# A ring of eight weight slots and rounds of eight experts in a hybrid decoder step

## The reference, cut to what matters

```
g_idx  = argmax(xf @ w_group + b_group)              # one of 4 groups
top 2 of the 8 experts of that group, by xf @ w_router + b_router
def expert_block(a):                                  # for each of the 32 experts
    gate, up = split(xb @ w_gate_up[e], 2)            # 1024 x 1024
    return (silu(gate) * up) @ w_down[e]              # 512 x 1024
y = sum over a token's two experts of weight * row
```

## Time and profile before

| what | value |
|---|---|
| median of 3 runs | 2447.42 us |
| the profiled execution's own time | 2444.9 us |
| its span | 2443.2 us |
| PE busy | 1804.6 us, 74% |
| DMA | 604.27 MB, mean 247 GB/s |
| experts of layer 0, on PE | 861.5 to 1420.2 us |
| experts of layer 1, on PE | 1868.4 to 2402.2 us |

### The profile page before, as it was taken

The page is one execution under the profiler, slowest core; times in us unless marked ns, Lnnn a source line. Parts: engine busy times, 40 slices in busy tenths (PEclk is TensorE's granted clock), DMA queues, the critical chain, the costliest instruction groups (busy, mean ns, idle before and its releaser), DMA issues. The chain is left out here.

```text
span 2443.2 us, 26085 instructions
## 1 busy us (share of the span) xinstructions
PE 1804.6 (74%) x8637; PEld 846.2 (35%) x8638; DVE 487.0 (20%) x989; ACT 300.4 (12%) x563; POOL 179.7 (7%) x167
## 2 busy tenths in 40 slices
PE   3779877368867478888888718999944788787682
PEld 1335333134433333333333204555442333332231
DVE  0010695332132201100000031121131010000003
ACT  1130111322101010010101012000020101010001
POOL 0000111001102200000000030000121000000004
PEclk8769989568688589999999968999967999899896
DMA  7992203907701277799999990010045999999994
GB/s 252 387 383 72 69 18 104 351 30 238 285 22 69 91 301 272 297 407 410 408 411 411 410 342 2 1 69 2 35 172 215 354 366 411 409 411 411 411 410 174
DMA packets 194115, 604.27 MB, mean 247 GB/s; under 512 B 15951, under 2 KB 18288, under 8 KB 193897
## 3 DMA queue, kind: packets, MB, share of 16 engines
q1 hardware_dynamic: 158064, 522.21, 55.1%
q10 hardware_dynamic: 25761, 46.50, 5.2%
q0 software_dynamic: 10208, 34.48, 4.0%
HBM read 551.57 MB, written 52.01 MB: 247 GB/s over the span
## 5 line engine op out<-in xcount | busy, mean ns | idle before, releaser
L780 PE MATMUL ps<-ring,W 128*64 128x512 f32 x2048 | 465.4, 605 | 55.5 <-issue 32.7
L793 PE MATMUL ps<-ring,W 128*64 128x512 f32 x1024 | 272.8, 680 | 52.0 <-DVE W L1591 47.2
L780 PEld LDWEIGHTS ps<-ring,W 128*64 128x64 f32 x2048 | 173.2, 139 | 335.7 <-issue 334.9
L909 ACT ACTIVATE W<-ps 128x512 f32<-128x512 f32 (+4 forms) x243 | 134.5, 568 | 973.5 <-PE ps L793 364.3
L1585 DVE TENSOR_TENSOR W<-W,ps 128x256 f32<-128x256 f32 x64 | 26.9, 421 | 796.4 <-ACT W L1175 796.4
L886 PE MATMUL ps<-hT,ring 128*128 128x512 f32 x384 | 170.7, 597 | 0.5 <-DVE W L1609 0.5
L793 PEld LDWEIGHTS ps<-ring,W 128*64 128x64 f32 x1024 | 91.0, 155 | 193.3 <-issue 193.3
L545 PE MATMUL ps<-ring,hT 128*128 128x512 f32 (+1 forms) x240 | 116.9, 646 | 1.9 <-DVE W L1292 1.9
L467 PE MATMUL ps<-ring,cT 128*32 128x512 f32 x384 | 75.8, 931 | 31.9 <-DMA ring<-in_w_ada_dram 31.7
L886 PEld LDWEIGHTS ps<-hT,ring 128*128 128x128 f32 x384 | 71.1, 190 | 80.9 <-issue 80.4
L1304 DVE SCALAR_TENSOR_TENSOR W<-W,prm 128x512 f32<-128x512 f32 x120 | 89.5, 817 | 0.0
(11 more groups left out here) (280 smaller groups left out, 1553.4 us busy)
## 6 DMA issues: line engine op xcount, KB each, us to landing
ring<-in_w_gate_up_dram SPq DMA_DIRECT2D x128, 2048.0 KB, 16.8
ring<-in_w_down_dram SPq DMA_DIRECT2D x64, 2048.0 KB, 17.0
ring<-in_w_ada_dram SPq DMA_DIRECT2D x24, 2048.0 KB, 19.7
x_rows<-X ACTq DMA_DIRECT2D x1, 18944.0 KB, 53.0
ring<-in_cache_k_dram SPq DMA_DIRECT2D x64, 256.0 KB, 3.0
W<-x_rows SPq DMA_DIRECT2D x32, 512.0 KB, 17.8
x_rows<-W ACTq DMA_DIRECT2D x128, 128.0 KB, 5.9
ring<-in_cache_v_dram POOLq DMA_DIRECT2D x48, 256.0 KB, 4.6
```

Source lines behind the costliest of these rows:

```text
L780: x = mm(ps[CAP * z:CAP * z + CAP, 2 + j, :], xt[:, k, :], at[:, :, 256 * z:256 * z + 256], start=(k == 0), stop=(k == KD - 1))
L793: x = mm(ps[CAP * z:CAP * z + CAP, 5 + j, :], ht[:, k % 2, CAP * (k // 2):CAP * (k // 2) + CAP], ring[:, 3 * j + 2, at:at + 512], start=(k ...
L909: return fn(out, src, ACT.Copy, **k)
```

## The change

The ring gets two more slots, `slots[6]` and `slots[7]`, of the same size, laid over the first 4096 columns of `Hb` and of `hT`. Parts go round the eight slots: part k of expert i of a round lies in slot (3 i + k) mod 8, which closes after 8 experts. So the loop of each engine becomes 4 rounds of 8 steps, without a written-out last round, and SP loads a part when the part eight places before it has been used. The two new slots get their first parts (expert number 2 of the order, its two gate/up halves) once the scatter has landed and the logits are made. To have no special last step, there is a 17th pair of rows in `x_rows`, which is fetched and turned and not used (PAIRS 17, and the region behind the experts starts P rows later, XB). The gate of the sample rows moves to `g2s`, in columns 4096 to 5119 of `Hb`. The six loads of w_in_c wait for the last users of slots 0 to 5 in the new order.

```diff
-PAIRS = E // 2
+PAIRS = E // 2 + 1
+XB = E * CAP + P
-XR = -(-(E * CAP + (XTRA + NB - 1) * XC) // P) * P
+XR = -(-(XB + (XTRA + NB - 1) * XC) // P) * P
+NRING = 8
+LOADS = 3 * E // NRING
+        slots = [ring[:, s, :] for s in range(NSLOT)] + [hflat[:, 0:SLOT], tflat[:, 0:SLOT]]
+        g2s = hflat[0:NS, SLOT:SLOT + D]
...
-            with eng.Fori(0, E // 4 - 1) as q:
-                quad(q)
-            quad(E // 4 - 1, last=True)
+            with eng.Fori(0, E // 8) as r:
+                for i in range(8):
+                    p, q = 4 * r + i // 2, i // 2 + 1
+                    step(8 * r + i, i, r, p, i // 2 % 2, (q % 2, 2 * r + q // 2, 4 * r + q) if i % 2 else None)
+
+        def place(i, k):
+            return divmod(3 * i + k, NRING)
...
+                def fetch(r, i, parts=(0, 1, 2)):
+                    for k in parts:
+                        before, part_before = divmod(3 * i + k - NRING, 3)
+                        sp.wait_ge(M[("g0_mm", "gu_mm", "down_mm")[part_before]], done(l, 8 * r + before))
+                        part(EG * (i % 4) + 2 * r + i // 4, k, place(i, k)[1])
+                        if k == 1 and i % 2 == 0:
+                            rows_in(4 * r + (i // 2 + 1), (i // 2 + 1) % 2)
...
                 layer_wait(sp, l, "disp", 32 * NT)
                 rows_in(0, 0)
                 rows_in(1, 1)
-                step(0, 0, 2 * EG, pair=(2, 0))
...
-                with sp.Fori(0, 6) as q:
-                    quad(q)
-                quad(6, last=True)
-                step(E - 3, 1, E - 1)
+                layer_wait(sp, l, "lg_mm", 1)
+                part(2 * EG, 0, 6)
+                part(2 * EG, 1, 7)
+                rows_in(2, 0)
+                fetch(0, 2, (2,))
+                for i in range(3, 8):
+                    fetch(0, i)
+                with sp.Fori(1, E // 8) as r:
+                    for i in range(8):
+                        fetch(r, i)
...
-                def landed(j, k, p):
-                    pe.wait_ge(slot_in[3 * j + k], p * 16 + (base_in[l][3 * j + k] + 16))
+                def landed(r, i, k):
+                    turn, s = place(i, k)
+                    pe.wait_ge(slot_in[s], r * 48 + (base_in[l][s] + 16 * turn + 16))
```

More of the change, by code:

```diff
@@ L213, in mod @@
             return modT[:, MODS * KD * l + KD * m:MODS * KD * l + KD * m + KD, :]
-        slot_in = [sem(f"slot_in{s}") for s in range(NSLOT)]
+        slot_in = [sem(f"slot_in{s}") for s in range(NRING)]
         v_in = [sem(f"v_in{j}") for j in range(2)]
@@ L250, in hybrid_step @@
         seq = 16 * NPG
-        in0 = [80 + 5 * seq] * 2 + [80, 80, 96, 80]
-        in1 = [in0[s] + 16 * PAIRS + (32 if s < 2 else 16) for s in range(NSLOT)]
+        in0 = [80 + 5 * seq] * 2 + [80, 80, 96, 80] + [0, 0]
+        in1 = [in0[s] + 16 * LOADS + (32, 32, 16, 16, 16, 16, 0, 0)[s] for s in range(NRING)]
         base_in = [in0, in1]
@@ L373, in experts @@
                         sp.wait_ge(S["bch_mm"], 4 * (s // 3 + 1))
-                    part(EG * (s // 3), s // 3, s % 3)
+                    part(EG * (s // 3), s % 3, s)
                 def rows_in(p, j):
@@ L392, in experts @@
                 rows_in(1, 1)
-                step(0, 0, 2 * EG, pair=(2, 0))
[L395 to L399, removed]
-                with sp.Fori(0, 6) as q:
-                    quad(q)
-                quad(6, last=True)
-                step(E - 3, 1, E - 1)
[L406 to L409, removed]
+                layer_wait(sp, l, "lg_mm", 1)
[8 more added lines that the diff above has]
+                        fetch(r, i)
             experts(0)
             winc = a["w_in_c"][0].rearrange("(k p) n -> p k n", p=P)
[L413 to L416, removed]
+            for s in range(NSLOT):
+                last, part_last = divmod(3 * E - NRING + s, 3)
+                sp.wait_ge(M[("g0_mm", "gu_mm", "down_mm")[part_last]], done(0, last))
+                col = D * (s % 3) + 512 * (s // 3)
+                load(s, winc[:, :, col:col + 512])
             woutc = a["w_out_c"][0].rearrange("(k p) n -> p k n", p=P)
@@ L774, in ffn, with gate_up @@
                 layer_wait(pe, l, "gate2_ev", 4)
-                def gate_up(xt, j, half, signal):
+                def gate_up(xt, i, half, signal):
+                    j, slot = i % 2, slots[place(i, half)[1]]
                     for k in range(4 * half, 4 * half + 4):
-                        at = ring[:, 3 * j + half, D * (k % 4):D * (k % 4) + D].rearrange("p (g f) -> p g f", g=2)
+                        at = slot[:, D * (k % 4):D * (k % 4) + D].rearrange("p (g f) -> p g f", g=2)
                         for z in range(2):
@@ L787, in h_turns, with down @@
                     x.then_inc(signal, 1)
-                def down(ht, j, signal):
+                def down(ht, i, signal):
+                    j, slot = i % 2, slots[place(i, 2)[1]]
                     for k in range(FE // P):
@@ L793, in down @@
                             x = mm(ps[CAP * z:CAP * z + CAP, 5 + j, :], ht[:, k % 2, CAP * (k // 2):CAP * (k // 2) + CAP],
-                                   ring[:, 3 * j + 2, at:at + 512], start=(k == 0), stop=(k == FE // P - 1))
+                                   slot[:, at:at + 512], start=(k == 0), stop=(k == FE // P - 1))
                     x.then_inc(signal, 1)
                 def pair_turns(lane, count, p):
-                    pe.wait_ge(x_in[lane], count * 16 + (16 * (PAIRS // 2) * l + 16))
+                    pe.wait_ge(x_in[lane], count * 16 + (16 * ((PAIRS + 1 - lane) // 2) * l + 16))
                     pe.wait_ge(M["xa_ok"], pdone(l, p - 1))
@@ L819, in one_pass @@
                         for half in range(2):
-                            landed(j, half, p)
+                            landed(r, i, half)
                             carry(pe)
                             for k in range(4 * half, 4 * half + 4):
-                                at = ring[:, 3 * j + half, D * (k % 4):D * (k % 4) + D].rearrange("p (g f) -> p g f", g=2)
+                                at = slots[place(i, half)[1]][:, D * (k % 4):D * (k % 4) + D].rearrange(
+                                    "p (g f) -> p g f", g=2)
                                 for z in range(4):
@@ L837, in one_pass @@
                                 x = mm(ps[XC * z:XC * z + XC, 5 + j, 0:256], hhT2[:, k, :],
-                                       ring[:, 3 * j + 2, at:at + 256], start=(k == 0), stop=(k == 3))
+                                       slots[place(i, 2)[1]][:, at:at + 256], start=(k == 0), stop=(k == 3))
                         x.then_inc(F["products"], 1)
@@ L1707, in ffn, with step @@
                 meet(pool, k0)
-                def step(n, j, p, lane, nxt=None):
+                def step(n, i, r, p, lane, nxt=None):
+                    j = i % 2
                     def one_pass(c):
```

58 lines of the change are left out of this document (23 added, 35 removed).

## The result

The changed kernel takes 2541.3 us (median, 2528.8 to 2546.0) against 2446.6 us (2438.1 to 2448.9) of the kernel before on the same chip: ratio 1.0386, interval 1.0337 to 1.0434. It is 95 us slower; 50 were forecast. The profiled execution spans 2544.2 us against 2443.2.

A forecast was written before the change was run, and what follows sets the result against it. It took DMA as setting the loops' pace (16.7 us an expert where it is the limit), PE close behind. Code stalls of 83.8 less 33.9 us of weight waits gave +50 on the profiled 2444.9, so 2497 us predicted, range 2420 to 2545.

The forecast's parts named there:

- The place of the decision: PE's code in the expert loops: a round of eight, 11 packets, is not kept and every round fetches it again.
- rival B: Much slower by code alignment: four stalls in a round instead of two, 66 us more, 2563 us; chance 0.10.
- the forecast's own case: Rounds of eight fetched again each time: 2497 us, from 2447 to 2535; chance 0.62.
- idle at issue, apart from jumps back: PE's code-fetch stalls within rounds of both loops: 12 more at 2.85 us, +34.2 us.
- six jumps back: PE's returns to the loop head, three a layer: 5.7 us each, 17.1 us a layer.
- longer products: PE's slow product behind each added stall: 1.28 us on the mean, none counted for jumps back.
- waits for weights: PE's waits for late weights in both loops go nearly whole: 8 + 25.9 = 33.9 us saved.
- two such stalls: In each round of eight on PE, one stall per half: 8 a layer against 2 before.
- the price of one: Each stall on PE in fresh code: 2.85 us idle plus 1.28 us of slower product, 4.1 us.
- What the ring is worth: Two more weight slots put DMA 10.2 us further ahead; alone worth 8 + 16.5 = 24.5 us.
- The small parts: 17th pair, x_rows fill, SP's new order and gate's new place: 0.1 us a layer for transposes, otherwise 0.
- ACT's, DVE's and POOL's longer rounds: Their code fetches on queue 14: unpriced, from 0 to one 2.85 us stall per jump back, taken as 0.

The follow-up runs named there:

- e1: Changed kernel with the ring put back to six slots, rounds of eight kept: 2533.7 us.
- e2: Changed kernel with further-pass code left out on the engines at steps where this input needs none, valid for this input only: 2397.4 us.
- e4: Kernel before with 56 never-executed products added to each step on PE, a round then 9.3 packets: 2770.2 us.
- e5: e2 with a ring of six slots instead of eight: 2435.5 us.
- e12: e6 with no instruction changed, TensorE's two loops moved to begin at the start of a packet: 2428.5 us.
- e9: Changed kernel with hint_back_edge=True on TensorE's loop, one instruction more at each round's head: 2511.1 us.
- e6: e2 with further-pass code at four steps of the round instead of two, the added ones never entered: 2468.1 us.
- e8: Kernel before with a one-column Silu on ACT ahead of the products' wait at each round's first step: 2439.1 us.
- e3: Kernel before with further-pass code kept at only one step of four in each layer: 2435.5 us.
- e11: Kernel before with the last four experts as an eighth round, an unused 17th pair, and e8's early Silu: 2425.6 us.
- e10: Changed kernel with further-pass code moved behind the round and reached by branches, valid for any routing: 2505.2 us.

## Why the prediction was right, and half as large as the effect

**The place of the decision was right.** The forecast stood on one step: a round of eight is about 11 packets, TensorE doesn't keep it, and each round fetches it again. It named 11 to 12 packets a round and some 130 in all; 13 (11 and 12 in the first rounds) and 127 came. e1, e2 and e4 show the cause: without the far slots nothing changes, without the unused code 144 us go, and with unused code added to TensorE alone the kernel before loses 326 us. That 11 packets are too many, and that they go out in the order in which they came in, was my assumption; no row of before shows either. The runs put the step between 5.8 and 7.6 packets. The kernel before, e5 and e2 jump back over 5.8, 5.7 and 5.7 packets without a fetch: none in 945 to 1350 us, in 1020 to 1391 us of e5, in 1006 to 1391 us of e2. A round that touches seven stays (e2, 37 packets), one that touches eight does not (e12, 96 packets).

**The number is half luck.** 2541.3 lies in the range, whose end of 2545 was drawn for rival B's sake; it lies above 2535, the high end of the forecast's own case, and the measured loss is almost twice the forecast's. The errors of the terms below mostly point the same way.

**The terms.** Over both loops, forecast and measured by the profiled executions:

| term | forecast | measured |
|---|---|---|
| idle at issue, apart from jumps back | +34.2 (12 more at 2.85) | +56.1 (32.7 to 88.8, 19 more) |
| six jumps back | +34.2 (5.7 each) | +55.4 (9.2 each) |
| longer products | +15.4 | +29.2 |
| waits for weights | -33.9 | -37.6 |
| waits for DVE before the second turn | 0 | -11.2 |
| the rest of the loops | 0 | +4.0 |
| sum | +50 | +95.9 |

**The number of stalls failed first.** "A round of eight has two such stalls": the price of one held, the number did not. The list of waits had 13 idle times at issue in the two loops before. Nine of them stand directly behind a further pass, one behind each of the nine experts that take one, as ahead of the product at 1225.52 in the earlier trace rows:
```profile
1220.82 1.94 PE L837 MATMUL ps<-ring,W 128*32 128x256 f32 x32 [0.38 <-DVE W L1577]
```
Seven of these nine fall in rounds whose code was all there, so they are no fetches, and the same nine are all that e2 has. The other four, 2.85 us each, are the four passages through fresh code of the earlier trace rows. In the changed kernel the nine are there again (24.0 us against 21.3), and apart from them and the jumps back there are 23 of 2.8 us. The forecast had two a round, 16; there were 2.9 a round. Rival B, with 2563 closer to the time than the forecast, had four a round, 32 in all; 23 is nearer to 16. Why it is about three was not tested.

**The jump back was mis-sized.** "I take the nearest rows, two idle times of 2.85": it is 9.2 us, above both the 5.7 taken and the 8.3 that I had as the upper end. e9 bears out that it is the fetch of the head: in four of six, where one packet was left in the idle time instead of two, 3.2 to 3.8 us were left.

**The longer products are the third.** PE's busy time rose by 29.2 us, of which the unused pair's turns are 2.2 (two times eight in 1.09 us). The rest, 27.0 us over 19 more stalls and six jumps back, is 1.1 us for each; the forecast took 1.28 for 12 stalls and nothing for the jumps, behind which all six products are slow. e6 and e12 show that this term isn't fixed by the number of packets, since it moved by 20 us in one loop with the fetches unchanged.

**What the ring is worth** where the code stays came out higher, 32 to 38 us instead of 24.5 (e5 against e2). The changed kernel has nothing of it: with PE so slow, six slots are enough (with six, e1, it takes 2534 us; with eight 2541). The waits for weights that the forecast took off go with either ring.

**The table loads were missed.** The forecast did not see that ACT loads its table once a round. The waits before the second turn fell by 11.2 us, 8.0 of it by six loads fewer (2.47 against 1.14). In the changed kernel, where PE sets the pace, this counts in full; in the kernels with short code it doesn't: moving all 14 loads is worth 5 to 9 us (e8), and e5 with six loads fewer is level with e3.

**The small parts held.** The first refill went out at 854 us, right behind the row fetches, and nothing of the SP's new order is seen in PE's waits. ACT's, DVE's and POOL's longer rounds, which I left unpriced, cost little: queue 14 has 64 packets instead of 33, and PE's waits for DVE before `down` (L790, L793 before) are 49.7 us instead of 47.2. The first product of layer 1 had an idle time of 5.87 at issue, counted above with the stalls.

## What to carry to other kernels

Count the packets that a loop's instructions touch, with code that is jumped over, before unrolling it further. On TensorE, in these runs, a round that touched seven (5.8 packets long) was free from the second time on, one that touched eight (7.6 long) was fetched whole in every round; nothing between was run. The step was worth 31 to 71 us by where the code lay (e12, e6), as much as or more than the 32 to 38 that two more slots of weights brought. Code written out once behind a loop is fetched too, five packets in layer 0; with a dummy turn in its place and the early table load, the kernel was 25 us faster than before (e11).

## What the runs showed of the hardware that was not expected

- A round that is too long by a packet or two is not one fetch dearer: all of it is fetched, 9 packets for a round of 7.6 (e6, e12).
- A jump back to a head that is gone costs 8.4 to 9.6 us of idle time (the changed kernel, e6's and e12's layer 1), an entry to far code 6.5 on the mean and up to 12.4 (e10); the stalls within a round that the code's length adds, 2.8 on the mean (23 in the changed kernel). In layer 0 of e6 and e12 no idle time at issue was above 3.7, though the packets came again there too; why is open.
- The same instructions in another place took 40 us less (e12), half of it in shorter products at a granted clock of 0.97 against 0.93 in layer 0, half in less idle time at issue, mostly in layer 1.
- A table load of 1.28 us stood on ACT's path in each round of a loop that calls no function but silu and copy, and a one-column call of that function ahead of the wait moved it off (e8).
- Behind each of the nine experts with a further pass PE stood idle for 1.7 to 3.1 us, and nothing in the profile ended it, in seven cases with all the round's code on the chip (the kernel before); why is open.
